# Products of constants into bank 7 on TensorE between the stages of a decoder step

## The reference, cut to what matters

```python
h = layer_norm(x, ln0)                              # entry
z = h @ w_in                                        # entry, features
ob = gmlp_gate(ub, vb, ...)                         # gate and pool
oc = pool_mix(xc, ...)
oa = stick_breaking(qa, ka, va, bias)               # attention, prompt and samples
od = gated_delta_rule(short_conv(qkv), ...)         # delta
h = layer_norm(ALPHA * h + concat(oa, ob, oc, od) @ w_out, ln1)   # residual "o"
mem_k, mem_v = mem_prompt @ xa_wk, mem_prompt @ xa_wv             # memory
c = cross_attention(h, mem_k, mem_v, xa_wq, xa_wo)  # queries, cross; residual "w" has xa_wo
h = layer_norm(ALPHA * h + c, ln2)
f = moe_ffn(h, w_router, ...)                       # route, experts (top 2 of 16)
y = layer_norm(ALPHA * h + f, ln3)                  # combine
```

## Time and profile before

| | |
|---|---|
| median of 3 runs | 1684.21 us (1684.13 to 1684.91) |
| the profiled execution | 1684.2 us, of which the span in the trace is 1682.4 us |
| TensorE busy | 1386.1 us (82% of the span), 9807 MATMUL rows |
| VectorE, ScalarE, GpSimd busy | 747.3, 448.1 and 207.7 us |
| mean granted clock of TensorE | 0.908 |

### The profile page before, as it was taken

The page is one execution under the profiler, slowest core; times in us unless marked ns, Lnnn a source line. Parts: engine busy times, 40 slices in busy tenths (PEclk is TensorE's granted clock), DMA queues, the critical chain, the costliest instruction groups (busy, mean ns, idle before and its releaser), DMA issues. The chain is left out here.

```text
span 1682.4 us, 24853 instructions
## 1 busy us (share of the span) xinstructions
PE 1386.1 (82%) x9807; PEld 936.7 (56%) x9808; DVE 747.3 (44%) x1132; ACT 448.1 (27%) x928; POOL 207.7 (12%) x196
## 2 busy tenths in 40 slices
PE   4999899778886997699698998969961998999900
PEld 2554799654444787488446987858821333333300
DVE  3321545237655564576401003346535443444368
ACT  1111424236765332322101214431110111111122
POOL 0000000003332751000000000000000110111056
PEclk9999899879997998599798999989985999999955
DMA  8110111022002100300351115430054495772153
GB/s 316 38 57 30 34 49 51 18 76 57 1 1 93 29 4 4 117 22 1 115 185 38 38 50 194 157 133 1 1 237 192 157 360 211 275 295 99 51 220 139
DMA packets 76946, 174.30 MB, mean 104 GB/s; under 512 B 12932, under 2 KB 40715, under 8 KB 70435
## 3 DMA queue, kind: packets, MB, share of 16 engines
q1 hardware_dynamic: 67387, 137.73, 23.2%
q0 software_dynamic: 5856, 21.24, 3.7%
q10 hardware_dynamic: 3600, 13.90, 2.0%
HBM read 142.27 MB, written 30.66 MB: 103 GB/s over the span
## 5 line engine op out<-in xcount | busy, mean ns | idle before, releaser
L2997 PE MATMUL bank<-arena,hT 128*64 x384 | 173.7, 606 | 11.3 <-DVE hT L3106 4.9
L2998 PE MATMUL bank<-arena,hT 128*64 128x512 f32 x384 | 173.7, 606 | 0.0
L471 PE MATMUL bank<-arena,hT 128*128 128x512 f32 (+3 forms) x432 | 141.1, 481 | 0.0
L2997 PEld LDWEIGHTS bank<-arena,hT 128*64 128x64 f32 x384 | 53.5, 140 | 124.2 <-issue 124.2
L3116 DVE COPY arena<-arena 128x4096 f32 x24 | 55.1, 2295 | 131.3 <-PE bank L2998 119.3
L471 PEld LDWEIGHTS bank<-arena,hT 128*128 128x128 f32 (+1 forms) x432 | 68.5, 184 | 72.8 <-issue 72.8
L2965 POOL DMA_INDIRECT hT<-tokens,row_token x24 | 40.3, 1678 | 440.4 <-PE bank L2982 229.8
L2111 PE MATMUL bank<-hT_rest,f_w_high 128*128 128x352 f32 x288 | 93.7, 326 | 0.0
L3021 PE MATMUL bank<-arena,hT 128*64 x192 | 87.5, 598 | 2.4 <-ACT hT L3061 2.4
L3023 PE MATMUL bank<-arena,hT 128*64 128x512 f32 x192 | 87.5, 598 | 0.0
L1577 PE MATMUL bank<-arena 64*64 64x64 f32 (+1 forms) x1920 | 68.6, 224 | 3.5 <-DVE arena L1950 3.0
(11 more groups left out here) (484 smaller groups left out, 2979.3 us busy)
## 6 DMA issues: line engine op xcount, KB each, us to landing
arena<-in_ex_wg_dram SPq DMA_DIRECT2D x16, 1024.0 KB, 7.5
arena<-in_ex_wu_dram SPq DMA_DIRECT2D x16, 1024.0 KB, 10.2
arena<-in_ex_wd_dram SPq DMA_DIRECT2D x16, 1024.0 KB, 12.3
expert_rows<-hT ACTq DMA_DIRECT2D x24, 512.0 KB, 5.2
arena<-in_cache_mem_k_dram SPq DMA_DIRECT2D x8, 1024.0 KB, 4.9
arena<-in_w_in_dram SPq DMA_DIRECT2D x12, 512.0 KB, 3.9
h<-in_x_prompt_dram SPq DMA_DIRECT2D x8, 512.0 KB, 8.9
arena<-in_w_in_dram SPq DMA_DIRECT2D x2, 2048.0 KB, 17.1
```

Source lines behind the costliest of these rows:

```text
L471: last = nc.tensor.matmul(ps[bank][0:r, 0:n], hT[:, k, i * P:i * P + r], wt[:, k, col:col + n], start=(k == 0), stop=(k == KC - 1))
L2997: nc.tensor.matmul(ps[UPB[u % 2]][0:LR, :], xT[:, u % 2, k, 0:LR], gate_up_of[:, bass.ds(slot, 1), :, k, :].rearrange("p a g f -> p (a g) ...
L2998: last = nc.tensor.matmul(ps[UPB[u % 2]][LR:P, :], xT[:, u % 2, k, LR:P], wB_gate_up[:, :, k, :], start=(k == 0), stop=(k == KC - 1))
```

## The change

A helper issues `n` matmuls of the identity block with the first 512 columns of the constants, all into bank 7, without a semaphore. It is called in ten places: 6 and 4 in entry, 9 and 24 in features (the 24 behind a wait for `cw_ok`), 9 or 13 at the start of a residual and 9 before its last transposes, 8 at the end of memory (behind a wait for `out_ok` 8), 5 in queries, 16 in experts.

```diff
--- before.py
+++ after.py
@@ -271,6 +271,13 @@
     return ap.partition_broadcast(n)
 
 
+def constant_products(c, n):
+
+
+    for _ in range(n):
+        c.nc.tensor.matmul(c.ps[7][:, :], c.K("ident"), c.const[:, 0:512], start=True, stop=True)
+
+
 def x_tile(T, i):
     if i < NT:
         return T['x_prompt'][0, i * P:(i + 1) * P, :]
@@ -444,6 +451,7 @@
         @block.tensor
         def _(pe):
             pe.wait_ge(const_in, 16)
+            constant_products(c, 6)
 
             def turn(i):
                 r = rows(i)
@@ -483,6 +491,7 @@
                 last.then_inc(k_turned, 1)
 
             turn(0)
+            constant_products(c, 4)
             pe.wait_ge(w_in, 48)
             for i in range(TILES):
                 if i + 1 < TILES:
@@ -576,6 +585,7 @@
 
         @block.tensor
         def _(pe):
+            constant_products(c, 9)
             for n in range(len(plan)):
                 pe.wait_ge(wl_ok, n + 1)
                 if n == 2:
@@ -598,6 +608,8 @@
                         last = nc.tensor.transpose(ps[7][:, m * 28:(m + 1) * 28], cs[0:28, m * P:(m + 1) * P],
                                                    K("ident", 28, 28))
                     last.then_inc(cw_mm, 1)
+            pe.wait_ge(cw_ok, 1)
+            constant_products(c, 24)
 
         @block.scalar
         def _(act):
@@ -2187,9 +2199,12 @@
                                                    h[0:r, i, (4 * q + k) * P:(4 * q + k + 1) * P], K("ident", r, r))
                     last.then_inc(turned, 1)
 
+            constant_products(c, 9 if split else 13)
             for i in range(TILES + 1):
                 if i < TILES:
                     product(i)
+                else:
+                    constant_products(c, 9)
                 if i >= 1:
                     transposes(i - 1)
 
@@ -2344,6 +2359,8 @@
                     pe.wait_ge(out_ok, 4)
                     for f in range(4):
                         turns(Km, f, 0, kturned, None)
+            pe.wait_ge(out_ok, 8)
+            constant_products(c, 8)
 
         @block.scalar
         def _(act):
@@ -2382,6 +2399,7 @@
 
         @block.tensor
         def _(pe):
+            constant_products(c, 5)
             for n in range(KC):
                 pe.wait_ge(low_ok, n + 1)
                 for g in range(GRP):
@@ -2967,6 +2985,7 @@
 
         @block.tensor
         def _(pe):
+            constant_products(c, 16)
             def lower(t):
 
                 return pe.value_load(c.tile_expert[0:1, bass.ds(2 * t, 1)], min_val=0, max_val=NE - 1)
```

## The result

The changed kernel takes **1698.99 us** (median of 4 executions, 1695.48 to 1699.29) against 1684.17 of the kernel before: the ratio is **1.0083**, 95% interval 1.0066 to 1.0100. It is slower by 14.8 us; the forecast was +13.6. The profiled execution took 1699.22 us, its span is 1697.4 us.

A forecast was written before the change was run, and what follows sets the result against it. TensorE was taken to bound most stages outside its pauses, with its clock at 0.50 for some microseconds behind them. Gains and overruns, priced at 0.86 us per product, summed to +13.6 on 1684.2: 1697.8 us, range 1689 to 1704.

The forecast's parts named there:

- The price: Every site: one product of constants is two f32 MATMULs of 0.43 us, 0.86 us at the higher clock, 1.71 at the lower.
- Entry: Six and four products around the first turn: a gain of 1.6 us, the middle between 2.8 and about nothing.
- Features' end: 24 products outlast the 12.14 us pause, TensorE ends at 343.3 and the whole next block waits: +8.2 us, between +6.0 and +9.3.
- its likelier case: Gate, behind features' end: the clock mostly falls again in the 6.1 us wait for the pool tables; only 0.6 us gained.
- Features' nine: Start of features: nine products take 7.7 us from 174.85, end at 182.6; a gain of 0.5 us.
- a loss of 0.8 if it falls: Features' nine products: the clock falls for a few microseconds at the end of entry; otherwise a gain of 0.9 us.
- Queries and experts: Memory's 8 with queries' 5 products: +2.3 us; 16 before the experts' first transposes: +5.2 us, between +3.0 and +6.5.
- Residuals: Residual "o": -1.1 us at the start, +1.2 before the last transposes; residual "w": +0.3 and -0.4.
- Half the price: Rival, all sites: one MATMUL takes 0.22 us, so products end inside the pauses; sum -12.8, 1671.4 us; chance 0.09.
- the barrier: Rival, features' end: the block's end doesn't wait for TensorE's queue, +2.8 in place of +8.2; 1692.1 us; chance 0.07.
- products that don't hold the clock: Rival: products of constants take up to 1.71 us each, +20 at features' end beyond the forecast, near 1740 us; chance 0.03.
- the last rival: Larger gains in gate (-2.9 for -0.6), entry (2.8) and experts (-2.3): sum still +7.8 us; chance 0.03.

## Why the prediction was right, and where it was not

*The price.* Right, and decisive: 0.86 us per product. From it the sign followed at every site but one.

*Entry.* -1.98 for -1.6. The clock was 0.50 from 19.6 to 23.0 us, within the four products, and up before the first projection. Five traces with the same ten products, this one among them, have -2.0 to -3.0, six without them +0.1 to -1.5.

*Features' end.* The step "all engines leave the block at about 343.5" measured 342.4, since entry had gained; relative to the work in front it is +8.76 against 8.8. The -0.6 for the clock behind it did not come: the clock fell again from 347.3 to 354.1, in the wait for the tables, as the prediction had for its likelier case.

*Features' nine.* Wrong in sign: +0.92 for -0.5. The step that failed is "they end at 182.6" without a look at the clock that they start with. It fell at 173.2, 0.3 us after they began, and came back at 176.6, so they took 9.1 us instead of 7.7 (the stretch in the kernel after: length, busy us and counts, granted clock):

```profile
173.20:176.60 3.40, 3.40 (x5) 1.33 (x4) 2.07 (x2) 3.40 (x4) 0.00 (x0) 0.50 0.31 102
```

The stage's other engines were 2 us early and could not use it. The text had this case, "a loss of 0.8 if it falls", and took the other side of it.

*Queries and experts.* Terms of the right sign, mis-sized: +2.8 for +2.3, and +3.9 for +5.2. In queries the first real product came 4.6 us later, as forecast, and the clock gave back 1.8 us, not 2.35. In experts the lower clock, up again at 1303.0, cost the first products 1.4 us and not the 2.3 counted, so `turn_x(0, 0)` stood 15.1 us behind the block's start and not 16. The rest of the difference is the stretch behind it, 0.3 us shorter than before where it was counted as somewhat longer. The clock fell again in the 3.85 us of waiting, as forecast, but that was not sure: with the 16 alone it stayed up over the same wait.

*Residuals.* "o" and "w" came within 0.7 us at each of their four places. The prediction had product 0 of "o" wait for the weights' pieces until 722.8 us at best. In both traces its 48 matmuls follow each other without idle time; it starts 0.9 us later against the stage's first cast, since the nine took 10.5 us, and ends 0.4 us earlier.

*The untouched stages.* The forecast put them at nothing, and in the full change they were near it: -0.23 and +0.16. The experiments show that this was not to be had from the argument. In three kernels (without the 24, the 16 alone, the 8 and 5 alone) cross was within 0.3 us of the kernel before, in eight others it took 2.7 to 7 us longer, and with half the columns 1.4 us less. So a sum of this kind can be wrong by 7 us in one stage, more than any of its terms but one.

*The sum.* That the total came within 1.2 us of the forecast is in part luck: the misses of the single terms, taken without their signs, add up to some 6 us, and cross could have added as much again. One sum in the prediction is also wrong as written: the stated ends of the terms add up to 1691.4 us at the low side, not 1689.

*The rivals.* Half the price is refuted by the pace (and shown to be what would have made the change a gain); the barrier by the DRAIN row; products that don't hold the clock by 20.76 us for 48 MATMULs, all at a granted clock of 1.00. Of the three larger gains of the last rival none came in the full change: the clock fell in gate, entry gave 2.0, and it fell in the experts' wait.

## What to carry to other kernels

Work that fills a pause has to be priced at its own data type and size and held against the pause, counted from the clock that it starts with: whatever reaches beyond the pause is paid in full, and the clock gives back at most half of the few microseconds behind it. The most expensive place is the end of a block, where a queue on one engine delays all others and the DMAs behind them. The same products, in counts cut to end before their data, made this kernel 0.5 to 0.7% faster.

## What the runs showed of the hardware

The time of a stage that no edit touches is not a constant: cross took 108.9 us with half the columns, at a granted clock of 1.00 throughout, 110.3 in the kernel before and 117.4 with the 24 alone, for the same 836 matmuls. Two rows of it, with half the columns and with the 24 alone once more:

```profile
993.09:1102.03 108.94, 96.27 (x836) 81.01 (x836) 35.43 (x62) 43.12 (x117) 3.61 (x2) 1.00 0.42 155
```
```profile
1009.45:1126.38 116.93, 102.96 (x835) 85.00 (x836) 35.41 (x62) 43.21 (x116) 3.61 (x2) 0.93 0.39 145
```

The time goes with how long its clock was 0.50 (none, 3.4 and 17.1 us) and, in the slowest, with a load that took 1.3 us longer; the slowest came back in a second series. Nor does one wait decide where the clock falls: over 3.85 us of idle time it fell in the full change and stayed at 1.00 with the 16 alone. A kernel with the 24 products alone was as slow (1698.5 and 1698.7) as the one with all 112 (1699.0), though the change without the 24 adds 4.5 us (1688.42 against 1683.89). A sum over sites is good to 5 to 7 us here, no matter how exact its terms are.
